# Two modulation chunks summed over k-tiles on VectorE, and the second one's loads later in the queue

## The chip, the cores and the metric

The kernel runs on one core of a Trainium2 chip. The metric is the device time of one execution in microseconds (us); for the kernel before it is 733.33 us, the median of three runs (732.9 to 733.6).

## The reference

Two transformer blocks follow one another on 256 tokens of width 1024, all in float32. What matters here is in the first:

```
mod = silu(c) @ w_ada + b_ada                    # [1, 6144]: sh1, sc1, g1, sh2, sc2, g2
u   = (rmsnorm(x) * norm_mix_g) * (1 + sc1) + sh1
z   = u @ w_in                                   # rq rk rv rg | dq dkv iq ik iw
y_ret = retention(rope(rq), rope(rk), rv, rg) @ w_ret_out
y_dsa = top-64 attention of 8 heads (dq, latent k and v, index scores) @ w_dsa_out
ga, gb = sigmoid(u @ w_gate + b_gate)
h   = x + g1 * ((ga * y_ret + gb * y_dsa) @ w_o)
u2  = (rmsnorm(h) * norm_ffn_g) * (1 + sc2) + sh2
h   = h + g2 * moe(u2)
```

The product `silu(c) @ w_ada` has one row and 6144 columns. It is computed in twelve chunks of 512 columns. Chunks 8 and 9 are sc2, the second scale; they are what the change touches, and their result is needed only for the router and the experts, much later.

## The kernel before, in words

**Pieces.** All large products run through a stream of "pieces". A piece is 512 KB of weights: two k-tiles of 128 rows by 512 columns, held as 128x1024 floats. `PIECES` is the list of them in order (`rg1` 0 to 3, `ga0` 0 to 3, `ga1`, `gb0`, and so on). For each piece SyncE issues the load into one of 8 slots of `raw` (L383) when the piece eight places before is done; ScalarE writes a rounded high part `hi` (L1415, 5 slots, so it may not run more than five pieces ahead of TensorE); VectorE writes the rest, `lo = raw - hi` (L1870, called "low" here); and TensorE does twelve 128x512 matmuls with them (L568 to L570: high by high, low by high, high by low). The float32 product is kept accurate in this way.

**Order.** There is no scheduler. Each engine has one program written out by hand, and runs it in order. In TensorE's program other products stand between the pieces; in VectorE's `lows_to(AT[...])` and in ScalarE's `his_to(AT[...])` say up to which piece the splitting goes before the next other step. So a step that takes longer holds back everything written after it on its engine, and whoever waits for that.

**Around the change** TensorE's program reads: `rg1` 0, `logits(1,0)`, `rg1` 1, `logits(1,1)`, `rg1` 2, product of chunk 8, `rg1` 3, `ga0` 0, spread of chunk 8, `ga0` 1, product of chunk 9, `ga0` 2, spread of chunk 9, `dsa_turn(1,0)` and `(1,1)`, `ga0` 3, `dsa_turn(1,2)` and `(1,3)`, `ga1` 0, `dsa_out(1)`, `ga1` 1, turns of rq, `ga1` 2, turns of rk, `ga1` 3, `ret_scores(0)`, `gb0` 0.

- `logits(1,g)` (L683) writes four heads of attention logits into the two banks `PM`. It waits until both banks are free, which for `logits(1,1)` means that VectorE has read those of `logits(1,0)` (L1940).
- After `logits(1,1)` VectorE takes the maxima (L1945), ScalarE does eight exponentials with their sums (L1465), VectorE the reciprocals of the sums (L1951), and GpSimd multiplies the eight heads by them, one 128x256 instruction each (`scale(1)`, L516, SBUF to SBUF). `dsa_turn(1,g)` (L695) transposes two heads; it waits for GpSimd's second, fourth, sixth and eighth head, and for its bank, which `prob` frees (VectorE L1961 for even g, ScalarE L1476 for odd g). `dsa_out(1)` (L724) needs all four `prob` copies.
- An `ada_product` (L637) is eight matmuls with `silu(c)` as 32 weight columns (one real, 31 zeros) against the chunk's 128x512 k-tiles, in four column groups of the array; ScalarE copies the bank to `SN` (L1455), `ada_spread` transposes `SN` in four 128x128 blocks (L646), and VectorE's `ada_end` sums the four values of each column (L1916).
- A chunk's weights are two loads of 1 MB, numbers 2n and 2n+1 (`ada(i)`, L407). For chunks 8 and 9 they go into the halves of `GS`, so 18 and 19 wait until 16 and 17 were used. Afterwards GpSimd's queue loads the gate bias into the same halves, for `gate("ga0")` and its like (L2043), which free the banks for the next columns.

The lines of the rule that the change replaces:

```
def ada_used(S, j):
    return S.ada.at("p", j if j < 8 else j | 1)
...
    if n in ADA_COL:
        for j in range(4):
            r = pe.transpose(PM[1][:, 128 * j:128 * j + 128], sn[:, 128 * j:128 * j + 128], ident)
```

Of the kernel before, what the change touches and what calls it, by code (L numbers as in the profile page):

```python
# [12 lines left out]
ALU = mybir.AluOpType  # L13
# [90 lines left out]
AT = {p: i for i, p in enumerate(PIECES)}  # L104
# [204 lines left out]
def signals(nc, ctx):  # L309
    S = Names()  # L310
# [19 lines left out]
    S.bias_in = [[land(f"bias{a}{tt}") for tt in range(2)] for a in range(2)]  # L330
    S.decay_in, S.gate_bias_in = land("decay"), land("gatebias")
    S.p_in, S.masks_in, S.final_gain_in, S.out_done = land("p"), land("masks"), land("fg"), land("out")
# [37 lines left out]
def ada_used(S, j):  # L370
    return S.ada.at("p", j if j < 8 else j | 1)


def sp_program(sp, T, S, I, out):
    q = Seat(sp)
# [62 lines left out]
    pieces(AT["rk", 0] - done[0])  # L438
    for i, then in ((8, ("rv0", 2)), (10, ("rv1", 2)), (12, ("rg0", 2)), (14, ("ga0", 0)), (16, ("ga0", 3)), (18, ("ro1", 3))):
        ada(i), ada(i + 1)  # L440
        pieces(AT[then] - done[0])
# [27 lines left out]
def pool_program(pool, T, S, I):  # L469
# [91 lines left out]
def pe_program(pe, T, S):  # L561
# [840 lines left out]
def act_program(act, T, S):  # L1402
# [458 lines left out]
def dve_program(dve, T, S):  # L1861
# [309 lines left out]
    lows_to(AT["ga1", 2])
    prob(S.dve_dsa, S.pe_dsa, "dsa", 1, 0)
    lows_to(AT["ga1", 3])
    prob(S.dve_dsa, S.pe_dsa, "dsa", 1, 2)
    lows_to(AT["gb0", 0])
    dsa_low(1)
    lows_to(AT["gb0", 1])
    gate("ga0")
    lows_to(AT["gb0", 3])

# [671 lines left out]
```

## Time and profile before

| what | value |
|---|---|
| median of 3 runs | 733.33 us (732.9 to 733.6) |
| the profiled execution, its own time | 732.7 us |
| its span in the profile | 731.4 us |
| TensorE matmul busy | 709.5 us (97%) |
| VectorE, ScalarE, GpSimd busy | 513.8 us (70%), 379.6 us (52%), 54.4 us (7%) |
| granted TensorE clock | 1.00 over the span |

The profile is of one execution. Busy times are the union of an engine's instructions; matmuls are pipelined, and in a row of full pieces one starts every 0.227 us though each is drawn 0.39 us long. Times in the timeline count from the span's start. Idle time before an instruction is put down to the one that released it last.

### The profile page before, as it was taken

How to read it: one execution, taken by the hardware profiler on the slowest of the kernel's cores; microseconds unless marked ns; L12 is line 12 of the kernel's file. 1: busy time of each engine (PE TensorE's matmuls, PEld its weight loads, DVE VectorE, ACT ScalarE, POOL GpSimd, SP SyncE). 2: the span in 40 equal slices, each digit the busy share in tenths (PEclk: the TensorE clock that was granted, in tenths of full speed). 3: DMA queues.
4: the chain of work that ended last, by engine and by line, in shares of the span. 5: the costliest groups of instructions: out<-in, count | busy, mean ns of one | idle time of the engine just before them, and what ended most of it. 6: DMA issues, size and time to landing. Idle time of an engine off the chain costs nothing.

```text
span 731.4 us, 9904 instructions
## 1 busy us (share of the span) xinstructions
PE 709.5 (97%) x3754; PEld 570.3 (78%) x3754; DVE 513.8 (70%) x759; ACT 379.6 (52%) x549; POOL 54.4 (7%) x68
## 2 busy tenths in 40 slices
PE   4999999999999999999999999999999999999997
PEld 2887666767888877888877777779888887888886
DVE  1456897536687774785668988887998665656854
ACT  3334435555436354474457877648533547644442
POOL 0002110240020000000000000011003400000000
PEclk9999999999999999999999999999999999999999
DMA  9999688588346931856589999945434574545541
GB/s 288 348 281 384 239 304 302 201 322 313 119 164 227 333 107 58 264 174 196 177 259 349 362 364 360 356 159 169 148 116 143 165 218 141 169 141 187 167 138 58
DMA packets 104894, 164.07 MB, mean 224 GB/s; under 512 B 10896, under 2 KB 53613, under 8 KB 104718
## 3 DMA queue, kind: packets, MB, share of 16 engines
q1 hardware_dynamic: 102942, 155.54, 64.4%
q0 software_dynamic: 1904, 7.90, 3.1%
q8 instruction: 30, 0.49, 0.3%
q14 instruction: 18, 0.15, 0.1%
HBM read 162.33 MB, written 1.08 MB: 223 GB/s over the span
## 4 chain that ended last, share of the span: by engine, by line
PE 83%; DVE 9%; ACT 3%; DMA 3%; issue 1%; SPq 0%; POOL 0%; ACTq 0%; DVEq 0%; POOLq 0%
PE p L568 23%; PE p L570 22%; PE p L569 22%; DVE s_rawr L1870 3%; PE p L637 2%; PE p L626 2%; PE p L1254 2%; DMA s_raw<-in_w_gate_dram 2%; PE p L683 1%; DMA s_GS<-in_w_ada_dram 1%; PE p L1083 1%; ACT s_hi L1415 1%; ACT s_L L1465 1%; PE p L707 1%; PE p L695 1%
## 5 line engine op out<-in xcount | busy, mean ns | idle before, releaser
L1870 DVE TENSOR_TENSOR s_rawr<-s_raw,s_hi 128x1024 fp32r<-128x1024 f32 x240 | 286.8, 1224 | 50.5 <-ACT s_hi L1415 50.0
L1415 ACT ACTIVATE s_hi<-s_raw 128x1024 fp32r<-128x1024 f32 x240 | 244.9, 1054 | 109.7 <-PE p L570 47.1
L568 PE MATMUL p<-s_hi,s_Ah 128*128 128x512 f32 (+1 forms) x464 | 187.4, 404 | 1.1 <-DVE s_rawr L1870 0.7
L570 PE MATMUL p<-s_hi,s_Al 128*128 128x512 f32 (+1 forms) x464 | 179.6, 387 | 0.0
L569 PE MATMUL p<-s_rawr,s_Ah 128*128 128x512 f32 (+1 forms) x464 | 179.4, 387 | 0.0
L568 PEld LDWEIGHTS p<-s_hi,s_Ah 128*128 128x128 f32 x464 | 87.2, 188 | 30.5 <-issue 10.2
L570 PEld LDWEIGHTS p<-s_hi,s_Al 128*128 128x128 f32 x464 | 87.1, 188 | 18.5
L569 PEld LDWEIGHTS p<-s_rawr,s_Ah 128*128 128x128 f32 x464 | 87.4, 188 | 16.0 <-issue 0.5
L568 PE MATMUL p<-s_hi,s_Bh 128*128 128x512 f32 x192 | 76.3, 397 | 0.5 <-DVE s_BI L2441 0.3
L570 PE MATMUL p<-s_hi,s_Bl 128*128 128x512 f32 x192 | 74.9, 390 | 0.0
L569 PE MATMUL p<-s_rawr,s_Bh 128*128 128x512 f32 x192 | 74.8, 390 | 0.0
L568 PE MATMUL p<-s_hi,s_Ch 128*128 128x512 f32 x104 | 42.3, 407 | 0.4 <-DVE s_rawr L1870 0.2
L568 PEld LDWEIGHTS p<-s_hi,s_Bh 128*128 128x128 f32 x192 | 36.1, 188 | 7.9 <-DVE s_rawr L1870 0.4
L570 PEld LDWEIGHTS p<-s_hi,s_Bl 128*128 128x128 f32 x192 | 36.0, 188 | 7.7
L569 PEld LDWEIGHTS p<-s_rawr,s_Bh 128*128 128x128 f32 x192 | 36.1, 188 | 7.1
L570 PE MATMUL p<-s_hi,s_Cl 128*128 128x512 f32 x104 | 40.7, 391 | 0.0
L569 PE MATMUL p<-s_rawr,s_Ch 128*128 128x512 f32 x104 | 40.6, 390 | 0.0
L568 PE MATMUL p<-s_Ah,s_hi 128*128 128x256 f32 x128 | 37.1, 290 | 1.4 <-DVE s_Al L1900 1.3
L569 PE MATMUL p<-s_Al,s_hi 128*128 128x256 f32 x128 | 36.2, 283 | 0.0
L570 PE MATMUL p<-s_Ah,s_rawr 128*128 128x256 f32 x128 | 36.1, 282 | 0.0
L1715 ACT ACTIVATE s_Ch<-p 128x256 fp32r<-128x256 f32 (+1 forms) x16 | 7.0, 438 | 44.6 <-PE p L1126 44.6
L568 PEld LDWEIGHTS p<-s_Ah,s_hi 128*128 128x128 f32 x128 | 24.4, 191 | 2.4 <-issue 1.7
(380 smaller groups left out, 854.3 us busy)
## 6 DMA issues: line engine op xcount, KB each, us to landing
s_raw<-in_w_in_dram SPq DMA_DIRECT2D x80, 512.0 KB, 4.8
s_raw<-in_w_exp_gate_dram SPq DMA_DIRECT2D x64, 256.0 KB, 4.0
s_raw<-in_w_exp_up_dram SPq DMA_DIRECT2D x64, 256.0 KB, 5.0
s_raw<-in_w_exp_down_dram SPq DMA_DIRECT2D x32, 512.0 KB, 5.5
s_GS<-in_w_ada_dram SPq DMA_DIRECT2D x12, 1024.0 KB, 7.4
s_raw<-in_w_gate_dram SPq DMA_DIRECT2D x16, 512.0 KB, 9.6
s_GS<-in_w_ada_dram SPq DMA_DIRECT2D x8, 512.0 KB, 8.9
s_raw<-in_w_ret_out_dram SPq DMA_DIRECT2D x8, 512.0 KB, 3.6
```

What stands on the lines that cost most here:

```text
L568: pe.matmul(o, xh, wh, start=start, stop=False)
L569: pe.matmul(o, xh, wl, start=False, stop=False)
L570: return pe.matmul(o, xl, wh, start=False, stop=stop)
L626: r = pe.transpose(PT[b][:, 256 * k + 128 * tt:256 * k + 128 * tt + 128], src(tt, k0 + k), ident)
L637: r = pe.matmul(bank[32 * j:32 * j + 32, :], T.CS[:, 4 * h + j, :], w[:, j, :], start=h == 0, stop=h == 1, tile_position=(0, 32 * j))
L683: r = pe.matmul(PM[h % 2][:, 256 * (j // 2):256 * (j // 2) + ns], qT[o:o + 64, h // 2, 128 * tt:128 * tt + 128], kT(h, ns), start=True, st ...
L695: r = pe.transpose(PT[b][:, c:c + 128], Lv[:, per * g + j, 128 * s:128 * s + 128], ident)
L707: r = pe.matmul(PM[0][:, 64 * h:64 * h + 64], Pv[:, h, 128 * s:128 * s + 128], v(h, s), start=s == 0, stop=s == tt)
L1083: r = pe.matmul(o, rows[:, tt, 128 * k:128 * k + 128], T.P[:, tt, s0:s0 + n], start=tt == 0 and rows is T.X2h, stop=tt == 1 and rows is T.X2l)
L1254: r = pe.matmul(PM[tt][:, nq * h:nq * h + nq], ka[:, h, 128 * tt:128 * tt + 128], qa[:, h, nq * tt:nq * tt + nq], start=True, stop=True)
L1415: act.activation(T.hi[:, i % NHL, :], T.raw[:, i % NRAW, :], ACT.Copy).then_inc(*S.hi(i))
L1870: dve.tensor_tensor(T.lo[:, i % NRAW, :], T.raw[:, i % NRAW, :], T.hi[:, i % NHL, :].bitcast(F32), ALU.subtract).then_inc(*S.lo_dve(i))
```

## The change

Chunks 8 and 9 leave TensorE's `ada_product` and ScalarE's `ada_copy`. A new VectorE helper, `ada_part`, multiplies each of the chunk's eight 128x512 k-tiles by its column of `silu(c)` and adds it up in `SN`: one `tensor_scalar`, then seven `scalar_tensor_tensor`, each waiting for the one before. `ada_spread` still transposes `SN`, and `ada_end` now sums 128 values of each column instead of 4. The parts are placed among VectorE's other steps (chunk 8: four k-tiles before `logits(1,0)`, four behind the low of `ga0` 2; chunk 9: 4, 2 and 2). TensorE's spread of chunk 9 moves from behind `ga0` 2 to behind `ga1` 1. Loads 18 and 19 move behind three more gate pieces in SyncE's queue and wait for VectorE's fourth and eighth k-tile of chunk 8 instead of for TensorE. The gate bias is loaded in two parts with a semaphore each: the first half when the fourth k-tile of chunk 9 is used, the second when the eighth is. The two small operations behind `ada_end(9)` move back with it.

```diff
 def ada_used(S, j):
-    return S.ada.at("p", j if j < 8 else j | 1)
+    return S.dve_ada.at("acc", j // 2, 4 * (j % 2) + 3) if 16 <= j < 20 else S.ada.at("p", j if j < 8 else j | 1)
...
-    for i, then in (... (14, ("ga0", 0)), (16, ("ga0", 3)), (18, ("ro1", 3))):
+    for i, then in (... (14, ("ga0", 0)), (16, ("ga1", 2)), (18, ("ro1", 3))):
...
-    q.wait_ge(*ada_used(S, 19))
     for w in range(2):
+        q.wait_ge(*ada_used(S, 18 + w))
         for tt in range(2):
-            pool.dma_start(T.GS[:, w, tt, :], ...).then_inc(*S.gate_bias_in(0))
+            pool.dma_start(T.GS[:, w, tt, :], ...).then_inc(*S.gate_bias_in[w](0))
...
-    uses("rg1", 2, 3, A, u)
-    ada_product(8)
-    uses("rg1", 3, 4, A, u)
+    uses("rg1", 2, 4, A, u)
...
-    uses("ga0", 0, 1, A, u)
+    uses("ga0", 0, 2, A, u)
     ada_spread(8)
-    uses("ga0", 1, 2, A, u)
-    ada_product(9)
     uses("ga0", 2, 3, A, u)
-    ada_spread(9)
     dsa_turn(1, 0), dsa_turn(1, 1)
...
         uses("ga1", h, h + 1, A, u)
+        if h == 1:
+            ada_spread(9)
...
     exps(S.act_dsa, S.dve_dsa, 1)
-    ada_copy(8)
...
-    ada_copy(9)
...
+    def ada_part(n, js):
+        for j in js:
+            h = j // 4
+            w, c = ada_place(T, 2 * n + h)[:, j % 4, :], T.CS[:, j, 0:1]
+            q.wait_ge(*S.ada_in[h].at(2 * n + h))
+            if j:
+                q.wait_ge(*S.dve_ada.at("acc", n, j - 1))
+                dve.scalar_tensor_tensor(out=T.SN[:, :], in0=w, scalar=c, in1=T.SN[:, :], op0=ALU.mult, op1=ALU.add).then_inc(*S.dve_ada("acc", n, j))
+            else:
+                q.wait_ge(*S.ada.at("s", n - 1))
+                dve.tensor_scalar(T.SN[:, :], w, c, None, ALU.mult).then_inc(*S.dve_ada("acc", n, j))
...
     lows_to(AT["ga0", 0])
+    ada_part(8, range(0, 4))
     logits(S.dve_dsa, S.pe_dsa, 1, 0, S.dve_dsa.at("bias", 1))
     lows_to(AT["ga0", 1])
     logits(S.dve_dsa, S.pe_dsa, 1, 1, S.dve_dsa.at("bias", 1))
     maxima(S.dve_dsa, 1)
     lows_to(AT["ga0", 3])
+    ada_part(8, range(4, 8))
     recips(S.dve_dsa, S.act_dsa, 1)
+    lows_to(AT["ga1", 1])
     ada_end(8)
+    ada_part(9, range(0, 4))
     lows_to(AT["ga1", 2])
+    prob(S.dve_dsa, S.pe_dsa, "dsa", 1, 0)
+    lows_to(AT["ga1", 3])
+    ada_part(9, range(4, 6))
+    prob(S.dve_dsa, S.pe_dsa, "dsa", 1, 2)
+    lows_to(AT["gb0", 0])
+    ada_part(9, range(6, 8))
+    dsa_low(1)
+    lows_to(AT["gb0", 1])
+    gate("ga0")
+    lows_to(AT["gb0", 3])
     ada_end(9)
```

**VectorE from the low of `rg1` 3 to the reciprocals.** Before (L1870 is a low, L1940 the logits, L1945 and L1947 the maxima, L1951 the reciprocals):

```order
L1870 TENSOR_TENSOR s_rawr<-s_raw,s_hi 128x1024
L1940 SCALAR_TENSOR_TENSOR s_L<-p,s_BI 128x2x256 x2
L1870 TENSOR_TENSOR s_rawr<-s_raw,s_hi 128x1024
L1940 SCALAR_TENSOR_TENSOR s_L<-p,s_BI 128x2x256 x2
L1945 TENSOR_REDUCE s_st<-s_L 128x8
L1947 TENSOR_SCALAR s_st<-s_st 128x8
L1870 TENSOR_TENSOR s_rawr<-s_raw,s_hi 128x1024 x2
L1951 RECIPROCAL s_st<-s_st 128x8
```

and now (the same lines are L1865, L1948, L1953, L1955 and L1959; L1914 and L1911 are `ada_part`):

```order
L1865 TENSOR_TENSOR s_rawr<-s_raw,s_hi 128x1024
L1914 TENSOR_SCALAR s_SN<-s_GS,s_CS 128x512
L1911 SCALAR_TENSOR_TENSOR s_SN<-s_GS,s_CS,s_SN 128x512 x3
L1948 SCALAR_TENSOR_TENSOR s_L<-p,s_BI 128x2x256 x2
L1865 TENSOR_TENSOR s_rawr<-s_raw,s_hi 128x1024
L1948 SCALAR_TENSOR_TENSOR s_L<-p,s_BI 128x2x256 x2
L1953 TENSOR_REDUCE s_st<-s_L 128x8
L1955 TENSOR_SCALAR s_st<-s_st 128x8
L1865 TENSOR_TENSOR s_rawr<-s_raw,s_hi 128x1024 x2
L1911 SCALAR_TENSOR_TENSOR s_SN<-s_GS,s_CS,s_SN 128x512 x4
L1959 RECIPROCAL s_st<-s_st 128x8
```

Four instructions of chunk 8 stand between a low and the first logits, and four more between the low of `ga0` 2 and the reciprocals.

**VectorE behind the reciprocals**, up to the second `prob` copy (L1961, now L1969). Before:

```order
L1916 TENSOR_REDUCE s_mcols<-p 128x4
L1870 TENSOR_TENSOR s_rawr<-s_raw,s_hi 128x1024 x3
L1916 TENSOR_REDUCE s_mcols<-p 128x4
L2168 TENSOR_TENSOR s_mcols<-s_mcols,s_VC 128x16
L2170 SCALAR_TENSOR_TENSOR s_mc<-s_mcols,s_VC 128x8
L1961 COPY s_PP<-p 128x512
L1870 TENSOR_TENSOR s_rawr<-s_raw,s_hi 128x1024
L1961 COPY s_PP<-p 128x512
```

and now:

```order
L1865 TENSOR_TENSOR s_rawr<-s_raw,s_hi 128x1024 x2
L1924 TENSOR_REDUCE s_mcols<-p 128x4
L1914 TENSOR_SCALAR s_SN<-s_GS,s_CS 128x512
L1911 SCALAR_TENSOR_TENSOR s_SN<-s_GS,s_CS,s_SN 128x512 x3
L1865 TENSOR_TENSOR s_rawr<-s_raw,s_hi 128x1024
L1969 COPY s_PP<-p 128x512
L1865 TENSOR_TENSOR s_rawr<-s_raw,s_hi 128x1024
L1911 SCALAR_TENSOR_TENSOR s_SN<-s_GS,s_CS,s_SN 128x512 x2
L1969 COPY s_PP<-p 128x512
```

Two lows stand ahead of the first `ada_end`, and chunk 9's first four k-tiles ahead of the first `prob` copy.

**SyncE's queue** (L383 a piece, L407 a modulation load), the difference:

```order
 L407 DMA s_GS<-in_w_ada_dram 128x4x512 x2
-L383 DMA s_raw<-in_w_gate_dram 128x2x512 x3
-L407 DMA s_GS<-in_w_ada_dram 128x4x512 x2
-L383 DMA s_raw<-in_w_gate_dram 128x2x512 x13
+L383 DMA s_raw<-in_w_gate_dram 128x2x512 x6
+L407 DMA s_GS<-in_w_ada_dram 128x4x512 x2
+L383 DMA s_raw<-in_w_gate_dram 128x2x512 x10
```

Loads 18 and 19 stand three pieces further back.

## Rows read from the trace of the kernel before

**Rows 1.** The page, engines: busy us, share of the span, instructions.

```profile
PE 709.5 (97%) x3754; PEld 570.3 (78%) x3754; DVE 513.8 (70%) x759; ACT 379.6 (52%) x549; POOL 54.4 (7%) x68
```

**Rows 2.** Timeline of TensorE: start us, duration us, engine, line, what, count.

```profile
144.72 1.13 PE L683 MATMUL p<-s_SM,s_T 64*128 64x256 f32 x8
145.78 0.50 PE L568 MATMUL p<-s_hi,s_Ah 128*128 128x512 f32 x1
...
150.58 0.50 PE L568 MATMUL p<-s_hi,s_Ah 128*128 128x512 f32 x1
...
153.47 0.39 PE L568 MATMUL p<-s_hi,s_Ah 128*128 128x512 f32 x1
...
156.19 0.60 PE L646 MATMUL p<-s_blob,s_SN 128*128 128x128 f32 x4
156.55 0.47 PE L568 MATMUL p<-s_hi,s_Ah 128*128 128x512 f32 x1
...
165.67 1.04 PE L695 MATMUL p<-s_blob,s_L 128*128 128x128 f32 x8
166.46 0.47 PE L568 MATMUL p<-s_hi,s_Ah 128*128 128x512 f32 x1
...
169.30 1.03 PE L695 MATMUL p<-s_blob,s_L 128*128 128x128 f32 x8
...
173.00 1.94 PE L724 MATMUL p<-s_PP,s_SM 128*64 128x512 f32 x8
```

**Rows 3.** Timeline of VectorE; in brackets idle time before, and its releaser.

```profile
141.85 1.23 DVE L1870 TENSOR_TENSOR s_rawr<-s_raw,s_hi 128x1024 fp32r<-128x1024 f32 x1 [2.65 <-ACT s_hi L1415]
142.99 1.28 DVE L1940 SCALAR_TENSOR_TENSOR s_L<-p,s_BI 128x512 f32<-128x512 f32 x2
...
145.90 1.29 DVE L1940 SCALAR_TENSOR_TENSOR s_L<-p,s_BI 128x512 f32<-128x512 f32 x2 [0.50 <-PE p L683]
147.22 2.29 DVE L1945 TENSOR_REDUCE s_st<-s_L 128x8 f32<-128x2048 f32 x1
...
155.26 1.23 DVE L1870 TENSOR_TENSOR s_rawr<-s_raw,s_hi 128x1024 fp32r<-128x1024 f32 x1 [4.42 <-ACT s_hi L1415]
...
163.31 2.59 DVE L1870 TENSOR_TENSOR s_rawr<-s_raw,s_hi 128x1024 fp32r<-128x1024 f32 x2 [6.30 <-ACT s_hi L1415]
```

**Rows 4.** Timeline of ScalarE: the first exponential, and the copy behind the eighth.

```profile
149.75 0.51 ACT L1465 ACTIVATE s_L<-s_L,s_st 128x256 f32<-128x256 f32 x1 [4.73 <-DVE s_st L1947]
...
153.70 0.58 ACT L1455 ACTIVATE s_SN<-p 128x512 f32<-128x512 f32 x1
```

**Rows 5.** VectorE's timeline at 75.92; then groups: busy us, mean ns, idle.

```profile
75.92 1.01 DVE L1987 SCALAR_TENSOR_TENSOR s_PP<-s_L,s_IW,s_PP 128x256 f32<-128x256 f32 x2
...
L2268 DVE TENSOR_TENSOR s_X<-s_X,s_ZC 128x512 f32<-128x512 f32 x4 | 2.8, 692 | 0.1
...
L2061 DVE TENSOR_SCALAR s_YR<-s_X,s_st 128x1024 f32<-128x1024 f32 x2 | 1.4, 750 | 10.0 <-POOL s_st L477 10.0
```

**Rows 6.** GpSimd's scalings and VectorE beside them: timelines, and single instructions (min/median/max ns, start).

```profile
127.98 1.23 DVE L1870 TENSOR_TENSOR s_rawr<-s_raw,s_hi 128x1024 fp32r<-128x1024 f32 x1 [1.23 <-ACT s_hi L1415]
...
L516 POOL TENSOR_SCALAR s_L<-s_L,s_st x1: 1634/1634/1634, 128.0 to 128.0; 128x128 f32<-128x128 f32 x1
...
156.70 7.23 POOL L516 TENSOR_SCALAR s_L<-s_L,s_st 128x256 f32<-128x256 f32 x8 [8.61 <-DVE s_st L1951]
...
L516 POOL TENSOR_SCALAR s_L<-s_L,s_st x1: 917/917/917, 163.0 to 163.0; 128x256 f32<-128x256 f32 x1
...
163.31 1.25 DVE L1870 TENSOR_TENSOR s_rawr<-s_raw,s_hi 128x1024 fp32r<-128x1024 f32 x1 [6.30 <-ACT s_hi L1415]
```

**Rows 7.** One VectorE instruction beside GpSimd's two-input add (ns, start).

```profile
L1987 DVE SCALAR_TENSOR_TENSOR s_PP<-s_L,s_IW,s_PP x1: 1384/1384/1384, 82.3 to 82.3; 128x256 f32<-128x256 f32 x1
```

**Rows 8.** DMA issues of 104 to 112 and 147 to 152 us: count, KB, us to landing.

```profile
s_GS<-in_w_ada_dram SPq DMA_DIRECT2D x1, 1024.0 KB, 5.1
...
s_raw<-in_w_gate_dram SPq DMA_DIRECT2D x1, 512.0 KB, 10.5
```

More of the change, by code:

```diff
@@ L330, in signals @@
     S.bias_in = [[land(f"bias{a}{tt}") for tt in range(2)] for a in range(2)]
-    S.decay_in, S.gate_bias_in = land("decay"), land("gatebias")
+    S.decay_in, S.gate_bias_in = land("decay"), [land(f"gatebias{w}") for w in range(2)]
     S.p_in, S.masks_in, S.final_gain_in, S.out_done = land("p"), land("masks"), land("fg"), land("out")
@@ L438, in sp_program @@
     pieces(AT["rk", 0] - done[0])
-    for i, then in ((8, ("rv0", 2)), (10, ("rv1", 2)), (12, ("rg0", 2)), (14, ("ga0", 0)), (16, ("ga0", 3)), (18, ("ro1", 3))):
+    for i, then in ((8, ("rv0", 2)), (10, ("rv1", 2)), (12, ("rg0", 2)), (14, ("ga0", 0)), (16, ("ga1", 2)), (18, ("ro1", 3))):
         ada(i), ada(i + 1)
@@ L521, in pool_program @@
     scale(1)
-    q.wait_ge(*ada_used(S, 19))
     for w in range(2):
+        q.wait_ge(*ada_used(S, 18 + w))
         for tt in range(2):
-            pool.dma_start(T.GS[:, w, tt, :], I["b_gate"][:, 1024 * w:1024 * w + 1024].broadcast_to([128, 1024])).then_inc(*S.gate_bias_in(0))
+            pool.dma_start(T.GS[:, w, tt, :], I["b_gate"][:, 1024 * w:1024 * w + 1024].broadcast_to([128, 1024])).then_inc(*S.gate_bias_in[w](0))
     q.wait_ge(*S.act_ret.at("yo", 3))
@@ L670, in ada_spread @@
     def ada_spread(i):
-        ada_sum(i, T.SN[:, :], S.act_ada.at(i))
+        ada_sum(i, T.SN[:, :], S.dve_ada.at("acc", i, 7) if i in (8, 9) else S.act_ada.at(i))
     def att_logits(done, name, tt, g, qT, kT, ready):
@@ L1914, in ada_end @@
             m, c = ADA_COL[n], 4 * (n % 2)
-            v = T.PM[1][:, :].rearrange("p (j g c) -> p j g c", j=4, g=4)[:, :, :, 0]
+            v = T.PM[1][:, :].rearrange("p (j g) -> p j g", j=4) if n > 7 else T.PM[1][:, :].rearrange("p (j g c) -> p j g c", j=4, g=4)[:, :, :, 0]
             dve.tensor_reduce(T.mcols[:, m, c:c + 4], v, AX.X, ALU.add).then_inc(*S.dve_ada(n))
@@ L2038, in gate @@
         w, n = int(name[1] == "b"), int(name[2])
-        q.wait_ge(*S.gate_bias_in.at(0))
+        q.wait_ge(*S.gate_bias_in[w].at(0))
         for tt in range(2):
@@ L2170, in dve_program @@
     dve.scalar_tensor_tensor(out=T.mc[:, 0, 8:16], in0=T.mcols[:, 3, :], scalar=1.0, in1=T.g_ffn, op0=ALU.add, op1=ALU.mult).then_inc(*S.dve_res("mod"))
[L2171 to L2179, printed above, removed]
     mv = st[:, 256:288].rearrange("p (t h a) -> p t h a", t=2, a=2)
```

## The prediction

> **What bounds the kernel now.** I read the shares first: TensorE is busy 97% of the span [rows 1], so its own program, in order, is the clock. What counts is TensorE time taken out, and every new wait put in. Then the timeline of TensorE around the change [rows 2]: it runs without a gap worth naming from 144.72 to 173.00, so nothing there is free for it. Last the same stretch on the engines that feed it. VectorE looks idle, 6.30 us ahead of 163.31 alone [rows 3], and that is where the change puts its work. But the idle time lies in a few places, while the steps between it hand over to TensorE, to ScalarE and to GpSimd. So the question is which of those steps the new work stands in front of.
>
> **What is saved.** From the start of `rg1` 2 (145.78) to the first `dsa_turn` (165.67) is 19.89 us [rows 2], with both products, the spreads, and small waits. Without products: a first piece behind a break takes 2.89 (150.58 to 153.47), the next ones 2.72 (153.47 to 156.19), a spread 0.36 (156.19 to 156.55), a piece between two breaks 2.84 (166.46 to 169.30) [rows 2]. The new program needs 2.89 + 3 x 2.72 + 0.36 + 2.84 = 14.25. That is 5.64 less; the spread of chunk 9 comes back behind `ga1` 1 for 0.36. **Gain: 5.3 us**, all of it on the path. ScalarE's two copies go too; they lie in front of a `hi` [rows 4], and the chain below counts that.
>
> **What VectorE gets.** No row shows a 128x512 multiply-add. A 128x512 instruction with two SBUF inputs takes 0.69; the scalar form of 256 columns took 1.01 for two dependent ones, 0.48 each and 0.05 between, where plain 256-column work would be some 0.06 shorter. I take 0.75, and 0.79 from one to the next. Bounds: 0.48, as if it were no dearer than the 256-column form, to 1.0 for twice that. The one-input form takes 0.75 for 1024 columns, so I take 0.5 for 512 [rows 5]. Four k-tiles of a new chunk are then 0.5 + 2 x 0.79 + 0.67 = 2.8 up to the next independent instruction, and four later ones 3 x 0.79 + 0.75 = 3.1 until the sum is there. The wider `ada_end` goes from 0.17 to about the 0.69 of a 512-column instruction; it stands behind the reciprocals.
>
> **First stall, `logits(1,1)`.** VectorE now does four k-tiles before it empties the banks of `logits(1,0)`. It began that at 142.99 and needed 1.28 [rows 3], so it was done at 144.27, 0.45 ahead of TensorE's 144.72 [rows 2]. Now it is done at 142.99 + 2.8 + 1.28 = 147.1. TensorE waits from 144.72 to 147.1: **2.4 us**. The low ahead of it waits for ScalarE, not for anything the change moves, so it stays at 141.85 [rows 3]. Bounds of this stall: 1.3 (units of 0.48) to 3.0.
>
> **Second stall, the spread of chunk 8.** It needs the second four k-tiles, which stand behind the low of `ga0` 2, and that `hi` stands behind ScalarE's exponentials. From the start S of `logits(1,1)`: VectorE's logits at S + 1.18 (145.90 against 144.72), maxima 1.32 later, the first exponential 2.53 later (149.75 against 147.22), eight of them 3.95 (to 153.70) [rows 2 to 4]; then the `hi` 1.05 and 0.05 to the low, 1.14 for that, and 3.1 for the k-tiles: S + 14.3. TensorE is there at S + 1.06 + 2.89 + 3 x 2.72 = S + 12.1. It waits **2.2 us**, until T = 161.4. Bounds: 1.0 to 3.1.
>
> **Third and fourth stall, GpSimd's scaling.** The reciprocals stand behind the k-tiles, so GpSimd starts at about T + 0.2. Before, it had VectorE idle beside it: eight instructions in 7.23 us, 0.9 each [rows 6]. Now VectorE is at work through all of it with instructions of two SBUF inputs: two lows, chunk 9's multiply-adds, two more lows. What that does is in rows 6: a scaling of 0.6 us that started at 128.0, as a low had begun at 127.98, took 1.63; it waited until the low ended. The low took its usual 1.23. The other way round, the low at 163.31 came 0.3 us into a scaling and took 1.25. So a scaling that meets a two-input VectorE instruction waits for its end, and then delays the next one by at most some 0.3. Step by step in time behind T, 0.8 for each scaling from when it gets through: the first waits for a low until 1.3, done 2.1; second 2.7 to 3.5; third, behind the one-input multiply, 3.8 to 4.6; fourth 4.9 to 5.7; fifth 5.9 to 6.7; sixth 7.0 to 7.8; seventh, behind the low of `ga1` 1, 8.4 to 9.2; eighth, behind the low of `ga1` 2, 10.3 to 11.1. TensorE wants the fourth at T + 0.06 + 0.36 + 2.84 + 0.4 = 3.7 and waits **2.0**. `ga0` 3 then starts at 6.15, `dsa_turn(1,2)` at about 9.1 (the `prob` copy is ready at 9.1), and `(1,3)` wants the eighth scaling at 9.5 at the latest and gets it at 11.1: **1.8** with the copy's 0.1. Bounds for the two together: 0.9 (GpSimd undisturbed, next part) and 6.8 (each blocks the other fully).
>
> The Trainium skill, SBUF — State Buffer, section "Who interferes with whom", has the rule: a VectorE instruction with two SBUF inputs and a GpSimd instruction that reads SBUF share a read interface, and the one that comes later is blocked for the other's whole instruction. By its full form VectorE would lose the same time as GpSimd; the 1.63 agrees with it, the 1.25 does not.
>
> **The loads.** Load 19 and `ga1` 2 behind it are issued at T + 0.1 and T + 1.1, when no other load is under way. One 1 MB load took 5.1 us, half a MB behind it adds about 1.4; it lands at about T + 6.7, and its low is wanted at 9.1 [rows 8]. At a landing of 10.5 as in rows 8 it would be late. Load 18 goes at about 146 and is wanted at T + 3.3. The gate bias follows GpSimd's last scaling, T + 11, is wanted for `gb0` 0 some 16 us later, and costs nothing unless it needs more than that. `ada_end(9)` stands behind the low of `gb0` 2 and has to be done for `ret_scores(0)`: by my count 25 against 27 behind T, so nothing, with little to spare.
>
> **Sum.** 2.4 + 2.2 + 2.0 + 1.8 - 5.3 = +3.1 us. Behind `ret_scores(0)` both programs are alike and TensorE is the clock again, so it stays. The profiled execution's own 732.7 becomes 735.8; it lies 0.6 below the median of the runs, so the forecast in those terms is 733.3 + 3.1 = **736.4**.
>
> **Rivals.**
> - GpSimd is not held up (its scalings slip between VectorE's instructions). Then the wait for the fourth is 0.2, the `prob` copy behind chunk 9's k-tiles costs 0.35 and the second one 0.35: 0.9 in place of 3.8, sum +0.2, **733.5**. For it: the lows at 163.31 were hardly touched; against it: the 1.63. It decides the sign: held up by less than 1.4 us in all, nothing would be measured.
> - The k-tiles are cheap or the first two stalls don't arise, so that VectorE's idle time does take the work. All of them gone gives 728.0; with units of 0.48 the first two are 1.3 + 1.0, and with GpSimd hardly disturbed 0.5 more: -2.5, **730.8**. For it: 4.42 and 6.30 us of idle on VectorE [rows 3]. Against it: none of this idle time lies ahead of `logits(1,0)`, and the chain over the exponentials is counted in rows.
> - Both block one another fully. A VectorE multiply-add took 1.38 in place of 0.48 beside GpSimd's two-input add [rows 7]. Then the fourth scaling is done at T + 6.9 and the eighth at 13.9 to 14.4, 6.8 in place of 3.8: +6.1, **739.4**. By the rule of the Trainium skill (SBUF — State Buffer) it would be this one.
> - `ga1` 2 lands 10.5 us behind its issue, at T + 11.6: its low, chunk 9's next two k-tiles and the `prob` copy end at T + 16, where `dsa_out(1)` would start at 14.4: 1.6 more, 738.0.
>
> **Chances.** Forecast 0.45, its own range 734.8 to 737.8. GpSimd undisturbed 0.20. Work hidden, wholly or in large part, 0.18. Full mutual blocking 0.12. Late landing 0.05. No change means within 0.2% here, 1.5 us, about what a measurement can tell. Slower: 0.45 + 0.12 + 0.05 = 0.62; same 0.20; faster 0.18. The range reaches from 730.5, which leaves half of the hidden cases below, to 739.4, which leaves the worse half of full blocking above.
>
> **What would show it.** In the new profile `logits(1,1)` starts near 147.1 with VectorE's L1948 as releaser; the first spread (L646) waits some 2.2 us for L1911; two `dsa_turn`s (L695) wait for GpSimd's scaling, whose eight instructions take about 11 us in place of 7.2, with single ones of 1.2 to 1.9. The multiply-adds last 0.75. If the scaling takes 7.2 and L695 waits for nothing, the largest term is wrong; if L683 starts at 144.7, the first.

## The result, and the profile after

The changed kernel takes 736.62 us (median of 6 runs, 736.52 to 736.8), the kernel before 733.47 us beside it: a ratio of 1.0044, 95% interval 1.0033 to 1.0056. It is slower by 3.2 us. The forecast was 736.4 us, slower, with 0.62. The profiled span went from 731.4 to 735.2 us.

The page of the changed kernel, engines and then the chain that ended last:

```profile
PE 706.2 (96%) x3722; PEld 569.4 (77%) x3722; DVE 526.0 (72%) x775; ACT 377.7 (51%) x547; POOL 58.0 (8%) x68
...
PE 78%; DVE 11%; ACT 5%; SPq 2%; POOL 2%; issue 2%; DMA 1%; ACTq 0%; DVEq 0%; POOLq 0%
```

TensorE has 3.3 us less of busy time than in [rows 1], and the kernel is slower. TensorE's share of the chain fell from 83% to 78%; VectorE, ScalarE and GpSimd came in. The time is in new waits. TensorE's timeline, in the place of [rows 2] (start us, duration, line, what, idle before and its releaser):

```profile
147.29 1.14 PE L683 MATMUL p<-s_SM,s_T 64*128 64x256 f32 x8 [2.39 <-DVE s_L L1948]
148.36 0.50 PE L568 MATMUL p<-s_hi,s_Ah 128*128 128x512 f32 x1
...
161.65 0.66 PE L646 MATMUL p<-s_blob,s_SN 128*128 128x128 f32 x4 [2.12 <-DVE s_SN L1911]
162.06 0.47 PE L568 MATMUL p<-s_hi,s_Ah 128*128 128x512 f32 x1
...
166.49 0.60 PE L695 MATMUL p<-s_blob,s_L 128*128 128x128 f32 x4
167.58 0.66 PE L695 MATMUL p<-s_blob,s_L 128*128 128x128 f32 x4 [0.49 <-POOL s_L L516]
167.99 0.47 PE L568 MATMUL p<-s_hi,s_Ah 128*128 128x512 f32 x1
...
170.84 0.60 PE L695 MATMUL p<-s_blob,s_L 128*128 128x128 f32 x4
172.91 0.63 PE L695 MATMUL p<-s_blob,s_L 128*128 128x128 f32 x4 [1.47 <-POOL s_L L516]
...
176.23 1.94 PE L724 MATMUL p<-s_PP,s_SM 128*64 128x512 f32 x8
```

This profile runs 0.11 us later than that of before already ahead of the change (the low of `rg1` 3 at 141.96 against 141.85 [rows 3]). `dsa_out(1)` starts at 176.23 against 173.00 + 0.11: 3.1 us later. The account for that stretch:

| place | loss, us | how read |
|---|---|---|
| `logits(1,1)` | 2.46 | 147.29 against 144.72 + 0.11 |
| spread of chunk 8 | 2.24 | 161.65 against 148.36 + 2.89 + 3 x 2.72 |
| the spread itself | 0.05 | 0.41 against 0.36 |
| `ga0` 2 | 1.59 | 162.06 to 166.49, 4.43 in place of 2.84 |
| second turn | 0.70 | 1.09 after the first, in place of half of 0.79 |
| fourth turn | 1.69 | 2.07 after the third, likewise |
| saved up to here | -5.64 | as in the prediction |
| sum | +3.1 | |

The spread of chunk 9 comes 0.4 us behind that: +3.5 at `ret_scores(0)`, where the forecast said +3.1. This is one pair of executions. Their spans differ by 3.8 us, 0.11 of it from ahead of the change, while the medians differ by 3.2; so the account is good to some tenths of a us, not to the second digit.

The row of `ga0` 2 was not foreseen. The windows there (PE, PEld, DVE, ACT, POOL busy, granted clock, DMA share, GB/s) show why it took longer:

```profile
160.00:162.00 2.00, 0.35 (x3) 0.35 (x4) 1.93 (x5) 2.00 (x3) 0.18 (x1) 1.00 0.00 0
162.00:164.00 2.00, 2.00 (x9) 1.67 (x8) 2.00 (x3) 0.55 (x1) 2.00 (x1) 0.71 0.55 108
164.00:166.00 2.00, 2.00 (x6) 1.53 (x5) 1.93 (x4) 0.00 (x0) 2.00 (x3) 0.50 1.03 399
166.00:168.00 2.00, 1.51 (x11) 1.08 (x10) 1.97 (x3) 0.00 (x0) 2.00 (x3) 0.93 0.97 320
```

The granted clock fell to 0.50, that is 1.2 GHz, from about 162.9 to 166.3, after TensorE had been idle at 144.9 to 147.3 and again at 159.5 to 161.6. Whether that costs anything is a question for the runs below.

VectorE in the same stretch, in the place of [rows 3]:

```profile
143.10 0.48 DVE L1914 TENSOR_SCALAR s_SN<-s_GS,s_CS 128x512 f32<-128x512 f32 x1
143.62 2.33 DVE L1911 SCALAR_TENSOR_TENSOR s_SN<-s_GS,s_CS,s_SN 128x512 f32<-128x512 f32 x3
145.87 1.28 DVE L1948 SCALAR_TENSOR_TENSOR s_L<-p,s_BI 128x512 f32<-128x512 f32 x2
...
158.49 3.11 DVE L1911 SCALAR_TENSOR_TENSOR s_SN<-s_GS,s_CS,s_SN 128x512 f32<-128x512 f32 x4
161.51 0.20 DVE L1959 RECIPROCAL s_st<-s_st 128x8 f32<-128x8 f32 x1
161.63 2.31 DVE L1865 TENSOR_TENSOR s_rawr<-s_raw,s_hi 128x1024 fp32r<-128x1024 f32 x2
163.85 0.68 DVE L1924 TENSOR_REDUCE s_mcols<-p 128x4 f32<-128x512 f32 x1
164.45 0.48 DVE L1914 TENSOR_SCALAR s_SN<-s_GS,s_CS 128x512 f32<-128x512 f32 x1
164.96 2.65 DVE L1911 SCALAR_TENSOR_TENSOR s_SN<-s_GS,s_CS,s_SN 128x512 f32<-128x512 f32 x3
167.54 1.21 DVE L1865 TENSOR_TENSOR s_rawr<-s_raw,s_hi 128x1024 fp32r<-128x1024 f32 x1
```

And GpSimd's eight scalings, first as one group, then five of them singly (ns, start), in the place of [rows 6]:

```profile
161.81 10.95 POOL L516 TENSOR_SCALAR s_L<-s_L,s_st 128x256 f32<-128x256 f32 x8 [11.15 <-DVE s_st L1959]
...
L516 POOL TENSOR_SCALAR s_L<-s_L,s_st x1: 2828/2828/2828, 161.8 to 161.8; 128x256 f32<-128x256 f32 x1
L516 POOL TENSOR_SCALAR s_L<-s_L,s_st x1: 1083/1083/1083, 164.6 to 164.6; 128x256 f32<-128x256 f32 x1
L516 POOL TENSOR_SCALAR s_L<-s_L,s_st x1: 920/920/920, 165.7 to 165.7; 128x256 f32<-128x256 f32 x1
...
L516 POOL TENSOR_SCALAR s_L<-s_L,s_st x1: 1963/1963/1963, 167.5 to 167.5; 128x256 f32<-128x256 f32 x1
...
L516 POOL TENSOR_SCALAR s_L<-s_L,s_st x1: 1521/1521/1521, 170.3 to 170.3; 128x256 f32<-128x256 f32 x1
```

10.95 us in place of 7.23. The first scaling took 2.83: it waited through two lows that followed one another without a gap (161.63 to 163.85), and got in when VectorE read PSUM. The fifth (167.5) waited through one low. But beside the dependent multiply-adds (164.96) GpSimd ran at its 0.92 from the third scaling on (the second, under way when they began, took 1.08), and the three of them took 2.65 in place of 2.33.

### The profile page after: what moved, and what is told of

Same layout as the page of the kernel before. It is cut to its first block, busy times and chain, and to the rows that moved or that the text cites. A ratio compares the mean times of both kernels' runs of the same rounds, so it can differ in the third digit from the quotient of the medians.

```text
span 735.2 us, 9855 instructions
## 1 busy us (share of the span) xinstructions
PE 706.2 (96%) x3722; PEld 569.4 (77%) x3722; DVE 526.0 (72%) x775; ACT 377.7 (51%) x547; POOL 58.0 (8%) x68
## 3 DMA queue, kind: packets, MB, share of 16 engines
HBM read 162.33 MB, written 1.08 MB: 222 GB/s over the span
## 4 chain that ended last, share of the span: by engine, by line
PE 78%; DVE 11%; ACT 5%; SPq 2%; POOL 2%; issue 2%; DMA 1%; ACTq 0%; DVEq 0%; POOLq 0%
PE p L568 22%; PE p L570 21%; PE p L569 21%; DVE s_rawr L1865 4%; PE p L1251 2%; PE p L626 2%; PE p L637 2%; POOL s_L L516 1%; ACT s_L L1462 1%; ACT s_hi L1412 1%; DMA s_raw<-in_w_in_dram 1%; PE p L683 1%; PE p L1080 1%; SPq L405 1%; DVE s_st L1953 1%
## 5 line engine op out<-in xcount | busy, mean ns | idle before, releaser
L1865 DVE TENSOR_TENSOR s_rawr<-s_raw,s_hi 128x1024 fp32r<-128x1024 f32 x240 | 286.6, 1224 | 44.1 <-ACT s_hi L1412 43.6
```

The lines of the kernel that those rows point to most:

```text
L1865: dve.tensor_tensor(T.lo[:, i % NRAW, :], T.raw[:, i % NRAW, :], T.hi[:, i % NHL, :].bitcast(F32), ALU.subtract).then_inc(*S.lo_dve(i))
```

## The experiments

My theory after this reading: four terms make the loss (k-tiles in front of `logits(1,0)`; the chain over the exponentials to the spread; GpSimd's scaling, late and held up; small waits for copies), the saving of 5.3 us is real, and the half-speed stretch only fills a wait that would be there anyway. Rivals: the moved loads cost by themselves; the saving was overcounted; the clock costs its own 1.6 us; VectorE is simply too full.

**e1, the k-tiles next to free.** All sixteen k-tile instructions cut to 16 columns (496 columns of chunks 8 and 9 are left out).

```diff
-dve.tensor_scalar(T.SN[:, :], w, c, None, ALU.mult)
+dve.tensor_scalar(T.SN[:, 0:16], w[:, 0:16], c, None, ALU.mult)
-dve.scalar_tensor_tensor(out=T.SN[:, :], in0=w, scalar=c, in1=T.SN[:, :], ...)
+dve.scalar_tensor_tensor(out=T.SN[:, 0:16], in0=w[:, 0:16], scalar=c, in1=T.SN[:, 0:16], ...)
```

> The changed kernel, with every one of the sixteen k-tile instructions on VectorE cut to 16 of its 512 columns (so 496 columns of chunks 8 and 9 are left out, and sc2 is not what the reference has); order, semaphores and loads stay. If VectorE's time in front of the logits, the spread and the scaling is what costs, both long waits and the half-speed stretch go, and only the saving is left: 5.3 us under the kernel before, about 728.2 us. If the loads behind three more pieces, or the two-part bias, cost by themselves, it stays near or above 733. If the saving of TensorE time was smaller than counted, it lies between.

Measured: 732.59 us, 0.9993 of the kernel before (0.9984 to 1.0003). The expectation missed by 4.4 us: the long waits at the logits and the spread did go (0.59 left at the logits, none drawn at the spread), and nearly nothing was gained. Its timeline, TensorE and then GpSimd:

```profile
163.02 0.66 PE L695 MATMUL p<-s_blob,s_L 128*128 128x128 f32 x4 [1.56 <-POOL s_L L516]
...
168.65 0.63 PE L695 MATMUL p<-s_blob,s_L 128*128 128x128 f32 x4 [1.77 <-POOL s_L L516]
```

```profile
157.77 10.73 POOL L516 TENSOR_SCALAR s_L<-s_L,s_st 128x256 f32<-128x256 f32 x8 [9.09 <-DVE s_st L1959]
```

GpSimd is held up as much as before, 10.73 us, though the multiply-adds are short: the lows alone do it, and each scaling that took much over 0.92 met one. TensorE, now early, waits 3.3 us for it. I had forgotten my own third term when I wrote the expectation. Counted as in the table above, e1 loses 0.7 at the logits, 0.2 at the spread and 1.8 and 2.0 at the turns, 4.6 in all, against 5.2 saved (5.64 less 0.44 for the spread of chunk 9). That leaves a gain of 0.6, and `ret_scores(0)` starts 0.55 us earlier than before. So nothing is left over for the moved loads.

**e2, scaling on ScalarE.**

```diff
-    scale(1)                                  # GpSimd
...
     his_to(AT["ga1", 1])
+    for h in range(8):                        # ScalarE, behind the reciprocals
+        act.activation(Lv[:, h, :], Lv[:, h, :], ACT.Copy, scale=st[:, 88 + h:89 + h])
```

> The changed kernel, with the eight scalings of the second half of the rows on ScalarE (0.49 us each) in place of GpSimd. If the waits of the two dsa_turns (0.49 and 1.47 us in the profile of the changed kernel) come from GpSimd being held up by VectorE, both go: 2.0 us less, about 734.6 us, and VectorE's multiply-adds of chunk 9 return from 0.86 to 0.75 us. If the turns wait for the late reciprocals only, or for the prob copies, the second wait stays and the time is 736 or more.

Measured: 733.73 us, 1.0011 (1.0001 to 1.002), against 1.0044 for the changed kernel: 2.4 us better. (In the two profiles `dsa_out(1)` starts 3.25 us earlier, 172.98 against 176.23; the intervals of the two ratios leave room for that.) No turn waits for a scaling; one waits 0.42 us for VectorE's `prob` copy:

```profile
161.65 0.66 PE L645 MATMUL p<-s_blob,s_SN 128*128 128x128 f32 x4 [0.55 <-DVE s_SN L1917]
...
164.89 1.03 PE L694 MATMUL p<-s_blob,s_L 128*128 128x128 f32 x8
...
169.08 1.09 PE L694 MATMUL p<-s_blob,s_L 128*128 128x128 f32 x8 [0.42 <-DVE s_PP L1975]
```

VectorE's multiply-adds of chunk 9 are back at 0.75. In this execution the clock was at half speed ahead of the spread, at 148.3 to 151.8. The spread still starts at 161.65, as in the changed kernel; only its wait is shorter (0.55 in place of 2.12). So the chain over the exponentials sets the spread, not TensorE.

**e3, chunk 8's first four k-tiles behind the maxima.**

```diff
     lows_to(AT["ga0", 0])
-    ada_part(8, range(0, 4))
     logits(S.dve_dsa, S.pe_dsa, 1, 0, S.dve_dsa.at("bias", 1))
...
     maxima(S.dve_dsa, 1)
+    lows_to(AT["ga0", 2])
+    ada_part(8, range(0, 4))
     lows_to(AT["ga0", 3])
```

> The changed kernel, with the first four k-tiles of chunk 8 moved from in front of logits(1,0) to behind the maxima and the low of ga0 1, where VectorE waits for ScalarE's exponentials. By the chain (logits(1,1), maxima, exponentials, hi, low, four k-tiles) everything behind logits(1,1) moves forward with it by the whole first wait, 2.4 us, and nothing else changes: the spread still waits some 2.1 us, the scaling is held up as before. About 734.2 us. If instead the first wait was hidden under a later limit (loads, GpSimd), nearly nothing is gained, 736. If the half-speed stretch behind the spread goes too and GpSimd's waits do not take its place, 732.6.

Measured: 734.46 us, 1.0014 (1.0005 to 1.0024), 2.2 us better than the changed kernel's 1.0044:

```profile
144.83 1.13 PE L683 MATMUL p<-s_SM,s_T 64*128 64x256 f32 x8
...
159.21 0.66 PE L646 MATMUL p<-s_blob,s_SN 128*128 128x128 f32 x4 [2.14 <-DVE s_SN L1911]
```

The first wait is gone, the spread's is the same 2.14 us and starts 2.4 earlier. The expectation held. The two waits are one behind the other on a chain, so the first one counts whole.

**e4, loads 18 and 19 back ahead of `ga0` 3.** `(16, ("ga1", 2))` in SyncE's table set back to `(16, ("ga0", 3))`.

> The changed kernel, with loads 18 and 19 back at their old place, ahead of ga0 3. Load 19 waits for the eighth k-tile at 161.6 us, so ga0 3 and all pieces behind it are issued only then. ga0 3 would land some 7 us later, its low would hold up VectorE behind it, and the prob copy for dsa_turn(1,2) with it: some 4 us slower than the changed kernel, about 741 us. If the place in the queue does not matter, 736.6.

Measured: 742.99 us, 1.0137 (1.012 to 1.0154), 6.8 us slower than the changed kernel where I expected 4.4 (5.1 between the profiled spans, and this execution was the fastest of its four). VectorE sat idle for the `hi` of `ga0` 3, and TensorE for its low:

```profile
169.59 1.23 DVE L1865 TENSOR_TENSOR s_rawr<-s_raw,s_hi 128x1024 fp32r<-128x1024 f32 x1 [7.48 <-ACT s_hi L1412]
```

```profile
170.87 0.80 PE L568 MATMUL p<-s_hi,s_Ah 128*128 128x512 f32 x1 [4.32 <-DVE s_rawr L1865]
```

A load that waits for a late step holds every piece behind it in the queue. The new place is needed; it is no cost of the change.

The run shows one thing more. With VectorE idle behind the reciprocals, GpSimd is back at 7.22 us, though it starts as late as in the changed kernel:

```profile
162.22 7.22 POOL L516 TENSOR_SCALAR s_L<-s_L,s_st 128x256 f32<-128x256 f32 x8 [11.16 <-DVE s_st L1959]
```

The first two turns then come 3.25 us behind the spread and take 1.25 us in place of 1.04. So for the second turn the late start alone costs some 0.2 us, and the rest of that stall is the hold-up by VectorE.

**e5, the reciprocals in front of chunk 8's second four k-tiles.** `recips(...)` and `ada_part(8, range(4, 8))` exchanged.

> The changed kernel, with the reciprocals in front of the second four k-tiles of chunk 8, so that GpSimd's scaling starts 3.1 us earlier, beside dependent multiply-adds (which let it through in the changed kernel's profile, 0.92 each, at 0.86 for the multiply-add in place of 0.75). The fourth scaling is then done at about 162.5 and the turn does not wait, the eighth at about 168 to 169, where the last turn wants it at 169: both waits of the turns go, 2.0 us, and the spread comes 0.4 later. About 1.6 us under the changed kernel, 735.0. If the turns' waits are not GpSimd's doing, no change; if multiply-adds block GpSimd as lows do, 736.6 or more.

Measured: 734.58 us, 1.0023 (1.0011 to 1.0034), 1.5 us better than the changed kernel; expected 1.6. GpSimd starts 3 us earlier against the spread and needs 9.34 us; no turn waits for it, the third waits 0.91 for the `prob` copy. The first scaling, which came 0.2 us into a multiply-add, took 1.30:

```profile
159.04 9.34 POOL L516 TENSOR_SCALAR s_L<-s_L,s_st 128x256 f32<-128x256 f32 x8 [8.13 <-DVE s_st L1959]
```

```profile
170.26 1.09 PE L695 MATMUL p<-s_blob,s_L 128*128 128x128 f32 x8 [0.91 <-DVE s_PP L1969]
```

Here the clock fell at about 146.8, as `logits(1,1)` began (146.67). The logits took 2.01 us in place of 1.13, and VectorE could read them only 2.04 us behind their start, not 1.18:

```profile
148.71 1.29 DVE L1948 SCALAR_TENSOR_TENSOR s_L<-p,s_BI 128x512 f32<-128x512 f32 x2 [1.06 <-PE p L683]
```

The spread comes 20.96 us behind the low of `rg1` 3 (141.34), in the changed kernel 19.69. Of these 1.27 us, 0.4 is the expected price of the new order; 0.86 is the logits at half speed. A fall of the clock on a step of the chain does cost.

**e6, work in the spread's wait.**

```diff
     uses("ga0", 0, 2, A, u)
+    q.wait_ge(*m_free[0])
+    for _ in range(16):
+        pe.transpose(PM[0][:, 0:128], ident, ident)
     ada_spread(8)
```

> The changed kernel, with sixteen 128x128 transposes of a constant into a free bank in front of the spread of chunk 8, some 1.5 us of work in the 2.1 us that TensorE waits there. If the half-speed stretch behind the spread comes from that idle time, it goes; but GpSimd's fourth scaling is then what the turn waits for, near 2.0 us in place of 0.49, so the time stays within 0.4 us of the changed kernel, 736.5. If the half speed costs its 1.6 us by itself, 735.0.

Measured: 737.2 us, 1.0061 (1.0044 to 1.0078). By the ratios that is 1.2 us slower than the changed kernel, where I expected a difference within 0.4, but the intervals overlap. In the profiled execution the clock fell at about 148.6, behind the first wait, and not at the spread, so the run does not tell what the transposes do to the clock. It tells what the half speed on `ga0` 2 costs. The spread ended later, `ga0` 2 ran at full speed, and the second turn started at 167.57, as it did in the changed kernel (167.58):

```profile
160.99 1.91 PE L878 MATMUL p<-s_blob 128*128 128x128 f32 x16
162.73 0.60 PE L646 MATMUL p<-s_blob,s_SN 128*128 128x128 f32 x4
...
167.57 0.66 PE L695 MATMUL p<-s_blob,s_L 128*128 128x128 f32 x4 [1.03 <-POOL s_L L516]
```

GpSimd's fourth scaling sets that start, whether TensorE comes to it slowly or waits for it.

**e7, e1 and e2 together.** K-tiles of 16 columns, scaling on ScalarE.

> The k-tile instructions cut to 16 columns as in the first run (496 columns of chunks 8 and 9 left out), and the scaling on ScalarE. In the first run the turns waited 1.56 and 1.77 us for GpSimd though VectorE's k-tiles cost next to nothing. If these waits are what kept the saving of TensorE time from showing, it shows now: 5.3 less 0.6 at logits(1,1) and 0.3 at the spread, about 4.4 under the kernel before, 728.7 us. If the saving was overcounted, 731 or more.

Measured: 730.02 us, 0.9962 (0.9947 to 0.9976). The scaling's move, worth nothing in the kernel before (e10), is worth 2.3 us here. The waits that remain are 0.6 at `logits(1,1)` and 1.0 at the third turn, for VectorE's `prob` copy; with them the expected 4.4 becomes 3.4, and 2.8 was measured. Counted as in the table, the losses are 0.7 at the logits, 0.2 at the spread, 1.2 at the third turn and 0.1 behind it, so 5.2 saved leaves 3.0; in the profile `ret_scores(0)` starts 3.05 us earlier than before. The saving is there.

**e8, all k-tiles at full width, in other places.** VectorE's order is now:

```diff
     lows_to(AT["ga0", 0])
-    ada_part(8, range(0, 4))
     logits(S.dve_dsa, S.pe_dsa, 1, 0, S.dve_dsa.at("bias", 1))
     lows_to(AT["ga0", 1])
     logits(S.dve_dsa, S.pe_dsa, 1, 1, S.dve_dsa.at("bias", 1))
     maxima(S.dve_dsa, 1)
-    lows_to(AT["ga0", 3])
-    ada_part(8, range(4, 8))
+    lows_to(AT["ga0", 2])
+    ada_part(8, range(0, 4))
     recips(S.dve_dsa, S.act_dsa, 1)
-    lows_to(AT["ga1", 1])
-    ada_end(8)
-    ada_part(9, range(0, 4))
-    lows_to(AT["ga1", 2])
+    lows_to(AT["ga0", 3])
+    ada_part(8, range(4, 8))
+    lows_to(AT["ga1", 1])
     prob(S.dve_dsa, S.pe_dsa, "dsa", 1, 0)
-    lows_to(AT["ga1", 3])
-    ada_part(9, range(4, 6))
+    ada_end(8)
+    ada_part(9, range(0, 4))
     prob(S.dve_dsa, S.pe_dsa, "dsa", 1, 2)
+    lows_to(AT["ga1", 3])
+    ada_part(9, range(4, 8))
     lows_to(AT["gb0", 0])
-    ada_part(9, range(6, 8))
```

On TensorE the spread of chunk 8 stands behind `ga0` 2, that of chunk 9 behind `ga1` 2. ScalarE scales four heads behind the `hi` of `ga0` 3 and four behind that of `ga1` 0, and does its first `prob` copy ahead of the `hi` of `ga1` 1.

> All k-tiles at full width, put where nobody waits: chunk 8's first four behind the maxima, then the reciprocals, the low of ga0 2, the other four; spread of chunk 8 behind ga0 2, of chunk 9 behind ga1 2; prob copies ahead of chunk 9's k-tiles where a turn needs them; scaling on ScalarE in two halves. If the four terms (k-tiles before the logits, chain over the exponentials, GpSimd's scaling, copies) are the whole loss, the 5.3 us of TensorE time show nearly whole: 728.3 us, at most 729.5 with small waits for lows. If VectorE or ScalarE are simply too full here, 731 or more.

Measured: 728.0 us, 0.9933 (0.9916 to 0.995), and in five more rounds (**e11**) 728.19 us, 0.993 (0.9917 to 0.9942). It beats the kernel before by 5.0 us and the changed one (**e12**, 736.79 us, 1.0046 with 1.0034 to 1.0058, on the same chip) by 8.6. TensorE of e8:

```profile
144.78 1.13 PE L682 MATMUL p<-s_SM,s_T 64*128 64x256 f32 x8
...
159.58 0.60 PE L645 MATMUL p<-s_blob,s_SN 128*128 128x128 f32 x4
160.01 1.04 PE L694 MATMUL p<-s_blob,s_L 128*128 128x128 f32 x8
...
163.64 1.03 PE L694 MATMUL p<-s_blob,s_L 128*128 128x128 f32 x8
...
167.62 1.94 PE L723 MATMUL p<-s_PP,s_SM 128*64 128x512 f32 x8 [0.21 <-ACT s_PP L1477]
```

No wait but one of 0.21 us, for ScalarE's copy. That copy stands behind the `hi` of `ga1` 2, for which ScalarE was idle 2.30 us until its load landed (166.02): what comes next in this order is the load behind load 19. VectorE does the same sixteen instructions as in the changed kernel; it is not too full.

> e8_best once more, in more rounds and beside the changed kernel on the same chip: 728.0 us, 0.993 of the kernel before.

> The changed kernel as it is, beside e11 on the same chip: 736.6 us, 1.004 of the kernel before.

The second profile of the changed kernel (e12) has the half-speed stretch in another place, behind the first wait, at 149.0 to 152.4. The spread comes at the end of the same chain, and the second turn as far behind it as in the first profile, 5.92 against 5.93 us:

```profile
162.47 0.66 PE L646 MATMUL p<-s_blob,s_SN 128*128 128x128 f32 x4 [0.59 <-DVE s_SN L1911]
...
168.39 0.66 PE L695 MATMUL p<-s_blob,s_L 128*128 128x128 f32 x4 [1.15 <-POOL s_L L516]
```

**e9, the order of e8 with the scaling on GpSimd.**

> The order of e8_best with the scaling left on GpSimd. The reciprocals now come at 153.9, so GpSimd starts 7.7 us earlier than in the changed kernel; it is still held up by four lows and slows the multiply-adds of chunk 8 by 0.1 each, but should finish the fourth scaling near 158.7 (wanted 160.4) and the eighth near 163.9 (wanted 164.1). If only lateness together with the hold-up costs, this is within 0.5 us of e8_best: 728.5 us. If the hold-up costs wherever the scaling runs beside VectorE, 730 or more.

Measured: 728.66 us, 0.9937 (0.9924 to 0.995). Its interval overlaps that of e8. GpSimd is still held up, but it starts while there is time, and no turn waits for it:

```profile
154.04 9.78 POOL L516 TENSOR_SCALAR s_L<-s_L,s_st 128x256 f32<-128x256 f32 x8 [6.05 <-DVE s_st L1958]
```

In this profile `dsa_out(1)` waits 1.15 us for ScalarE's copy, in e8's 0.21. The copy stands again behind the `hi` of `ga1` 2, whose load landed at 167.00. Load 19, ahead of it in the queue, waits for chunk 8's last multiply-add, and beside GpSimd the four took 3.67 us in place of 3.11. So a part of the hold-up may reach TensorE by way of the loads; the times of e8 and e9 are too close to show it.

**e10, the kernel before with the scaling on ScalarE.**

> The kernel before, with nothing changed but the scaling of the second half of the rows on ScalarE. There the turns at 165.7 us do not wait for the scaling (GpSimd ends it at 163.9 beside an idle VectorE), so it should gain nothing: within 0.4 us of the kernel before. If ScalarE's scaling is a gain of its own, then part of what e2, e7 and e8 showed is not the end of a hold-up: 732 or less.

Measured: 733.07 us, 0.9995 (0.9986 to 1.0004): nothing, as expected. So what e2 gained is the end of GpSimd's late and held-up scaling, and not a gain of ScalarE.

## Why the prediction was right

**The saving, 5.3 us: right.** e8 has all of it but small waits, 5.0 us.

**The unit, 0.75 and 0.79: right.** The three multiply-adds at 143.62 took 2.33, which is 2 x 0.79 + 0.75; the one-input form took 0.48 where I took 0.5.

**First stall, 2.4: 2.39 idle.** The mechanism is the one named, with L1948 as releaser, and e3 takes it away for 2.2 us.

**Second stall, 2.2: 2.12 idle, 2.24 in the account.** T came out at 161.6, forecast 161.4. e2, e3 and e12 show that it is the chain: the spread keeps its place when TensorE comes later (e2, e12), and comes 2.4 us earlier when the chain starts earlier (e3).

**Third and fourth, 2.0 and 1.8: the sum right, the inside partly wrong.** The account has 1.59 + 0.70 and 1.69. The fourth scaling was done at T + 5.9 (forecast 5.7) and the eighth at T + 11.1 (11.1). But I let the first scaling in between the two lows at T + 1.3; it got in only behind both, 0.9 later. And I counted some 0.3 for VectorE at each scaling and one wait of GpSimd for each multiply-add; in fact a multiply-add lost 0.1, the first behind a low 0.2, and GpSimd next to nothing. The two errors cancelled, and that is luck. (The fourth stall, 11.1 - 9.5 + 0.1, is 1.7 and not 1.8 by the prediction's own rounded numbers.) e2 shows most of the term: its profile is 3.25 us ahead of the changed kernel's at `dsa_out(1)`, the medians 2.4. What is left there is mostly the `prob` copy.

**What it did not have: the clock.** Two waits of over 2 us were forecast, and a fall of the granted clock behind them was not. It took 1.6 us on `ga0` 2. It changed nothing in the sum, because that stretch lay in front of a wait that was due to be 2.0 us: 1.59 + 0.70 is the third stall in another dress (e6, e12). In another order it is a cost: in e5 the fall met `logits(1,1)` and put 0.86 us on the chain.

**The total.** 3.1 was forecast and 3.2 measured between the medians, but 3.5 at `ret_scores(0)` and 3.8 in the span between the two profiles. That the medians hit within 0.1 is in part luck; the terms are good to some tenths.

**The rivals.** "GpSimd is not held up", which decides the sign, is refuted by 10.95 us in place of 7.23, and by e2 and e4. "The k-tiles are cheap" was tried outright in e1, and gave 0.5 us in place of the 2.5 that I had put on it. The step of that rival that failed is its last term, "with GpSimd hardly disturbed 0.5": TensorE, being early, waited 3.3 us for GpSimd. "Both block one another fully" did not come: by it the fourth scaling would have been done at T + 6.9 and the eighth past T + 13.9. The Trainium skill, SBUF — State Buffer, section "Who interferes with whom", says that the later of the two is blocked for the other's whole instruction. For GpSimd the trace agrees (2.83 and 1.96 in place of 0.92). For VectorE it does not: a multiply-add of two SBUF inputs that meets a 0.92 us scaling took 0.85 to 0.87 in place of 0.75, and 0.97 once. "`ga1` 2 lands late" did not come in the changed kernel either: VectorE was idle 0.49 for its `hi` at 169.85, that `hi` (168.76) had stood behind ScalarE's `prob` copy and not waited for a load, and no turn waited for either.

**Left open.** When a scaling gets in between two lows. In the changed kernel and in e3, e6 and e12 it waited for both (2.83 us); in e1, e5 and e9 it got in behind the first, and the second low took 1.41 to 1.42 us in place of 1.22. From e1, a scaling and then the low:

```profile
L516 POOL TENSOR_SCALAR s_L<-s_L,s_st x1: 1967/1967/1967, 158.7 to 158.7; 128x256 f32<-128x256 f32 x1
```

```profile
L1865 DVE TENSOR_TENSOR s_rawr<-s_raw,s_hi x1: 1419/1419/1419, 159.9 to 159.9; 128x1024 fp32r<-128x1024 f32 x1
```

The scaling came some 0.2 us into the first low where it waited for both, and within 0.1 us of its start where it did not. Whether that decides it, no run shows.

And what exactly brings the clock down: it fell behind the first wait in five profiles (e2, e4, e5, e6 and e12), behind the second in one (the changed kernel's first), at the turns in one (e3), and once more in e4, from about 168.6, within its wait of 4.3 us, to 175.4. It did not fall in this stretch in e1, e7, e8, e9, e10 and e11, whose single waits there were 1.8 us or less.

## What to carry to other kernels

Idle time of an engine is not free room: ask what stands behind the place where the new work goes, on that engine and on those it releases. The same sixteen instructions cost 3.2 us at the places of the change and gave 5.0 us (4.6 with the scaling left on GpSimd) when they stood behind the maxima, while another engine was busy with the exponentials, and behind every copy that TensorE needed soon. A busy engine 3% from full gains only what its feeders can follow: when it becomes early, look for the next thing that now comes late (here a GpSimd scaling whose fourth head was ready at 160.4, 5.7 us ahead of its turn; it came to start 5.1 us later and to take 3.7 us longer), and start that first.

## What the runs showed of the hardware

- A GpSimd scaling of 0.92 us that met one low of VectorE (two SBUF inputs) took 1.96 to 1.99 us where it came as the low began. Behind two lows in a row it took 2.83 us in four profiles; in three others it got in after the first, and the second low lost 0.2 us. Beside a row of dependent multiply-adds, which have 0.04 us between them, it ran at 0.92, once they were both under way, and each multiply-add lost 0.1 us.
- In the profiles with waits of 2.1 to 2.4 us the granted clock was 0.50 for some 3.5 us, not at once and not at the same place in each execution: two profiles of the same kernel have it at 162.9 to 166.3 and at 149.0 to 152.4, with some 1.6 us lost on the pieces there. In e4 a second stretch lasted 6.8 us. Where TensorE had to wait behind the stretch anyway, the loss was inside that wait (e6, e12); where it fell on a step that others waited for, it was not (e5, 0.86 us).
- A 128x512 float32 multiply-add with both tensors in SBUF takes 0.75 us, 0.79 from one to the next when dependent, against 0.69 for a plain two-input instruction [rows 5].
